# Moving the accumulation of two modulation vectors from the second attention to the expert query projection

## The reference, cut to what matters

```python
mod = cond @ ada_w[i] + ada_b[i]            # 1024 -> 6 * 1024
sh1, sc1, g1, sh2, sc2, g2 = jnp.split(mod, 6, axis=-1)
h = modulate_2(rms_norm_2(x, norm_g[i, 0]), sh1, sc1)      # h * (1 + scale) + shift
...
x = x + (1 + g1)[:, None, :] * rms_norm_2(y, norm_g[i, 1])
h = modulate_2(rms_norm_2(x, norm_g[i, 2]), sh2, sc2)
```

## Time and profile before

| | |
|---|---|
| median of 3 runs | 1780.07 us |
| the profiled execution | 1779.83 us |
| its span, first to last instruction | 1778.0 us |
| mean granted TensorE clock | 0.965 of full speed |
| PE busy | 1684.4 us, 95% of the span |
| DVE busy | 1225.7 us, 69% |
| ACT busy | 916.1 us, 52% |
| POOL busy | 567.1 us, 32% |
| read from device memory | 337.87 MB, 191 GB/s over the span |

### The profile page before, as it was taken

One profiled execution on the slowest core, in us unless ns is written; L12 is line 12 of the kernel. 1 busy time (PEld: TensorE's weight loads), 2 busy tenths in 40 slices (PEclk: granted clock), 3 DMA queues, 4 the chain that ended last, 5 costly groups with the idle time before them and its releaser, 6 DMA issues.

```text
span 1778.0 us, 32337 instructions
## 1 busy us (share of the span) xinstructions
PE 1684.4 (95%) x11292; PEld 1506.1 (85%) x11292; DVE 1225.7 (69%) x2236; ACT 916.1 (52%) x1747; POOL 567.1 (32%) x230
## 2 busy tenths in 40 slices
PE   2998899999999999999999999998899999789998
PEld 1985799999999998788888878966799999579997
DVE  5466508869808983877777767759578877646665
ACT  1445445455459994455455454257644445554443
POOL 0681278989985555000000005401310005130000
PEclk8899899999999999999999999888899998999999
DMA  8664455565553334988888664353477864035563
GB/s 326 220 208 166 143 185 171 179 182 181 181 177 116 118 108 159 325 288 286 288 293 291 209 194 125 106 209 124 154 240 278 279 219 142 25 119 179 188 189 107
DMA packets 98426, 341.14 MB, mean 192 GB/s; under 512 B 12147, under 2 KB 16003, under 8 KB 98340
## 3 DMA queue, kind: packets, MB, share of 16 engines
q1 hardware_dynamic: 93988, 336.01, 56.9%
q10 hardware_dynamic: 4352, 4.02, 0.7%
HBM read 337.87 MB, written 1.07 MB: 191 GB/s over the span
## 4 chain that ended last, share of the span: by engine, by line
PE 86%; DVE 6%; ACT 3%; DMA 3%; issue 2%; ACTq 0%; SPq 0%; DVEq 0%
PE banks L617 25%; PE banks L618 25%; PE banks L619 24%; PE banks L902 3%; DMA arena<-in_ada 1%; PE banks L784 1%; PE banks L758 1%; DMA ada_ring<-in_ada 1%; DVE arena L1577 1%; PE banks L797 1%; PE banks L681 1%; ACT arena L1233 1%; DVE arena L1684 1%; PE banks L741 1%; PE banks L688 1%
## 5 line engine op out<-in xcount | busy, mean ns | idle before, releaser
L570 POOL TENSOR_TENSOR weights_low<-ring,weights_high 128x1024 fp32r<-128x1024 f32 x226 | 566.9, 2519 | 1029.5 <-DVE ht_low L1652 625.8
L1194 ACT ACTIVATE weights_high<-ring 128x1024 fp32r<-128x1024 f32 x480 | 505.6, 1054 | 508.6 <-PE banks L619 479.5
L617 PE MATMUL banks<-ht_high,weights_high 128*128 128x256 f32 x2008 | 582.2, 290 | 8.2 <-DVE ht_low L1652 6.0
L618 PE MATMUL banks<-ht_low,weights_high 128*128 128x256 f32 x2008 | 571.9, 285 | 0.0
L619 PE MATMUL banks<-ht_high,weights_low 128*128 128x256 f32 x2008 | 571.7, 285 | 0.0
L617 PEld LDWEIGHTS banks<-ht_high,weights_high 128*128 128x128 f32 x2008 | 389.1, 194 | 14.0 <-issue 11.3
L618 PEld LDWEIGHTS banks<-ht_low,weights_high 128*128 128x128 f32 x2008 | 389.2, 194 | 2.7
L619 PEld LDWEIGHTS banks<-ht_high,weights_low 128*128 128x128 f32 x2008 | 388.6, 194 | 0.0
L1632 DVE TENSOR_TENSOR weights_low<-ring,weights_high 128x1024 fp32r<-128x1024 f32 x254 | 310.5, 1223 | 39.5 <-ACT weights_high L1194 34.4
L617 PE MATMUL banks<-weights_high,ga_parts 128*128 128x512 f32 x504 | 198.0, 393 | 6.5 <-DVE ga_parts L1935 6.5
L618 PE MATMUL banks<-weights_low,ga_parts 128*128 128x512 f32 x504 | 197.2, 391 | 0.0
(11 more groups left out here) (255 smaller groups left out, 2315.6 us busy)
## 6 DMA issues: line engine op xcount, KB each, us to landing
ring<-in_stream SPq DMA_DIRECT2D x490, 512.0 KB, 3.5
arena<-in_ada SPq DMA_DIRECT2D x88, 512.0 KB, 3.9
ada_ring<-in_ada SPq DMA_DIRECT2D x56, 512.0 KB, 4.4
arena<-bias_rows ACTq DMA_DIRECT2D x1, 2048.0 KB, 11.6
X<-in_x SPq DMA_DIRECT2D x1, 1024.0 KB, 6.1
out<-X SPq DMA_DIRECT2D x4, 256.0 KB, 2.0
arena<-arena ACTq DMA_DIRECT2D x8, 127.5 KB, 3.8
arena<-in_norm_final SPq DMA_DIRECT2D x1, 512.0 KB, 4.7
```

The costliest lines, as they stand in the source:

```text
L570: pool.tensor_tensor(WL[:, c % SLOTS, :], ring[:, c % SLOTS, :], WH[:, c % HIGHS, :], ALU.subtract)\
L617: pe.matmul(out, wh, xh, start=start, stop=False, **kw)
L618: pe.matmul(out, wh, xl, start=False, stop=False, **kw)
L1194: act.activation(WH[:, c % HIGHS, :], ring[:, c % SLOTS, :], ACT.Copy).then_inc(S["high_ready"], 1)
```

## The change

The 16 pieces of vectors 12 and 13 are loaded and added beside the projection `wq` instead of beside the second attention. SP issues one of them behind each chunk from the ninth on (`chunk["wq"] + SLOTS`), into the two slots `ADA_WQ`. DVE adds them in one run behind `shift_banks(1)` and in front of the first `top16`. PE sums both accumulators with `ada_columns` right behind the sub-key scores, with a wait on the last piece in front, and `mod_columns([12, 13], 3)` takes the sums behind DVE's last `top16` work. From `norm_transpose(3)` the call goes away. The accumulators and slots lie at other places of the arena, and the sums calls behind are renumbered, with their banks.

```diff
+ADA_WQ = [A_P, A_P + D]
+A_ACC_WQ = [A_XN, A_XN + D]
-ADA_BEFORE = dict(start=0, qk1=2 * DB, mixer1=3 * DB, out1=4 * DB, peer=5 * DB, layer2=6 * DB, mixer2=12 * DB, mlp2=14 * DB)
+ADA_BEFORE = dict(start=0, qk1=2 * DB, mixer1=3 * DB, out1=4 * DB, wq=5 * DB, peer=7 * DB, layer2=8 * DB, mlp2=14 * DB)
...
@@ SP @@
-            ahead = chunk["out1"] + SLOTS + 4
+            load_chunks(chunk["out1"] + SLOTS + 4, chunk["wq"] + SLOTS + 1)
+            for k in range(2 * DB):
+                load_ada(k, ADA_WQ, ADA_BEFORE["wq"] + k - 1 if k >= 2 else None, 12 * DB + k, "ada_wq")
+                load_chunk(chunk["wq"] + SLOTS + 1 + k)
+            ahead = chunk["wq"] + SLOTS + 1 + 2 * DB
...
-            for i in range(2 * DB):
-                load_ada(i, ADA_LAYER3, ADA_BEFORE["mixer2"] + i - 1 if i >= 2 else None, 12 * DB + i, "ada3_slot")
-                if 1 <= i <= SLOTS:
-                    load_chunk(chunk["out2"] + i - 1)
+            load_chunks(chunk["out2"], ahead)
...
@@ PE @@
+            pe.wait_ge(S["ada_used"], ADA_BEFORE["peer"])
+            ada_columns([A(first, D) for first in A_ACC_WQ], 3)
...
-            norm_transpose(3, lambda: summed_3(ADA_BEFORE["mlp2"], (12, 13), 6))
+            norm_transpose(3)
...
@@ DVE @@
+            for k in range(2 * DB):
+                ada_piece(k, ADA_BEFORE["wq"] + k, "ada_wq", ADA_WQ, A(A_ACC_WQ[k // DB], D), 1)
...
+            mod_columns([12, 13], 3)
...
-                if step % 3 != 2:
-                    i = step // 3 * 2 + step % 3
-                    ada_piece(i, ADA_BEFORE["mixer2"] + i, "ada3_slot", ADA_LAYER3, A(A_ACC3[12 + i // DB], D), 1)
...
-                mod_columns([[12, 13], [14, 17], [15, 16]][k], 6 + k)
+                if k:
+                    mod_columns([[14, 17], [15, 16]][k - 1], 6 + k)
```

More of the change, by code:

```diff
@@ L218 @@
 A_ACC2 = [(i + 1) * D for i in range(6)]
-A_ACC3 = {12: A_SPARE, 13: A_WIN + D, 15: A_WIN, 16: A_WIN + D, 14: A_WIN + 2 * D, 17: A_WIN + 3 * D}
+ADA_WQ = [A_P, A_P + D]
+A_ACC_WQ = [A_XN, A_XN + D]
+A_ACC3 = {15: A_WIN, 16: A_WIN + D, 14: A_WIN + 2 * D, 17: A_WIN + 3 * D}
 ADA_ORDER = [*range(14), 15, 16, 14, 17]
-ADA_ROWS = [A_Y, A_ACC + 5 * D, A_P, A_XN, A_P, A_P, A_P, A_P]
-ADA_BEFORE = dict(start=0, qk1=2 * DB, mixer1=3 * DB, out1=4 * DB, peer=5 * DB, layer2=6 * DB, mixer2=12 * DB, mlp2=14 * DB)
+ADA_ROWS = {0: A_Y, 1: A_ACC + 5 * D, 4: A_XN, 6: A_P}
+ADA_BEFORE = dict(start=0, qk1=2 * DB, mixer1=3 * DB, out1=4 * DB, wq=5 * DB, peer=7 * DB, layer2=8 * DB, mlp2=14 * DB)
 def two_blocks(nc, a):
@@ L349, in xt @@
             return banks[:, xt_bank(n, b), (b % 2) * T:(b % 2 + 1) * T]
-        SUM_BANK = {0: 5, 1: 5, 2: 7, 3: 5, 4: 7, 5: 3, 6: 7, 7: 7, 8: 6}
-        ROW_CALLS = [0, 1, 3, 5]
+        SUM_BANK = {0: 5, 1: 5, 2: 7, 3: 5, 4: 5, 5: 7, 6: 3, 7: 7, 8: 6}
+        ROW_CALLS = [0, 1, 4, 6]
         def gated(j):
@@ L867, in summed_1 @@
             def summed_1():
-                pe.wait_ge(S["ada_used"], ADA_BEFORE["peer"])
+                pe.wait_ge(S["ada_used"], ADA_BEFORE["wq"])
                 ada_columns([ACC1[:, v, :] for v in range(3, 5)], 2)
@@ L943, in _ @@
             pe.wait_ge(S["ada_used"], ADA_BEFORE["layer2"] + 6 * DB)
-            ada_rows([ada_acc[:]], 3)
+            ada_rows([ada_acc[:]], 4)
             for j in range(NKEYS - SLOTS, NKEYS - LEAD):
@@ L947, in _ @@
                 if j == NKEYS - 8:
-                    ada_turned(1, 3)
+                    ada_turned(1, 4)
                 if j == NKEYS - 5:
@@ L966, in rope @@
                     if u == 2:
-                        pe.wait_ge(S["mod_ready"], 6)
+                        pe.wait_ge(S["mod_ready"], 7)
                     x = RAW[:, raw % 3, :]
@@ L1035, in summed_2 @@
                 ada_row_half(layer2_rows, 2, 0)
-                ada_columns([A(first, D) for first in A_ACC2[:2]], 4)
+                ada_columns([A(first, D) for first in A_ACC2[:2]], 5)
             pe.wait_ge(S["gate_rows_taken"], 2)
@@ L1040, in _ @@
             pe.wait_ge(S["rope_loaded"], 16)
-            roped_product("nsa", 16, ROPES2, 0, 2, lambda: ada_turned(4, 5))
+            roped_product("nsa", 16, ROPES2, 0, 2, lambda: ada_turned(4, 6))
             for t in range(TT):
@@ L1435, in _ @@
                      NKEYS - 5: [NKEYS - 1]}
-            take_ada(1, 3)
+            take_ada(1, 4)
             for j in range(NKEYS - SLOTS, NKEYS - LEAD):
@@ L1455, in _ @@
             scaled(2)
-            take_ada(4, 5)
+            take_ada(4, 6)
             used(chunk["v"] + NKEYS - 1)
@@ L1994, in _ @@
                 if j == NKEYS - 7:
-                    mod_columns([5], 3)
+                    mod_columns([5], 4)
                     spread_gate(1)
@@ L2023, in rope @@
                     dve.tensor_tensor(dst(i), t1, t2, ALU.add).then_inc(S["rope_done"], 1)
-            mod_columns([6, 7], 4)
+            mod_columns([6, 7], 5)
             scale_column(2, branch_row(2))
@@ L2031, in _ @@
                 dve.tensor_scalar(X[:, t, :], ZN[:, t, :], small[:, 32 + t:33 + t], None, ALU.mult)
-            mod_columns([*range(8, 12)], 5)
+            mod_columns([*range(8, 12)], 6)
             scale_column(3, branch_row(3))
```

## The result

The changed kernel took 1787.5 us in the median of its first seven runs (1784.0 to 1792.9), the kernel before 1779.6 us (1774.4 to 1781.8) beside it. The ratio is 1.0048, with a 95% interval from 1.0029 to 1.0067: slower by 5 to 12 us, 8 us in the middle. Twelve more runs on another occasion gave 1787.2 us and 1.0046 (1.0026 to 1.0067), beside 1778.9 us. Single executions of one kernel spread by far more than the 1 or 2 us named ahead: the kernel before from 1772.4 to 1789.4 us in 35 runs of one occasion. The profiled execution took 1787.53 us, its span is 1785.7 us.

What follows compares the result with a forecast made beforehand. PE was taken to bound the kernel (86% of the span). Wait 7.3, sums 3.7 and clock 2.0, less 5.0 for the attention and 0 for normalisation 3, gave +8.0 us: 1788 us, range 1776 to 1797.

Steps and rivals of the forecast that it cites:

- the wait: Behind the sub-key scores, PE waits for the last piece's add, done at 280.3 us: 7.3 us, bounds 0 and 17.
- the clock: Behind the query projection, wait and sums with little matmul work lower PE's clock: 2.0 us lost, bounds 0 and 5.4.
- The attention: Second attention without the pieces: 3.4 us less waiting for DVE plus 1.6 us of clock, 5.0 us gained; bounds 1 and 12.4.
- Normalisation 3: The sums were hidden behind a wait for DVE's normalised rows, so removing them gives 0; range -0.5 to +1 us.
- the rival that they keep pace: Query projection: landing and adding stay under 5.76 us, so no wait and no clock fall; 1771 or 1776 us; chance 0.16.
- The formula for a transfer: Piece transfers: 2.0 us plus bytes at 436 GB/s, 3.2 us for 512 KB; the prediction let rows of 4.4 to 5.6 decide.
- an aside: Query projection: locking at every chunk makes POOL's 2.40 us plus 1.1 us slower than PE's 2.88, starving PE before the scores.
- both engines lock each other at every chunk: Query projection: DVE and POOL block each other, interval 4.1 us, wait 17.0 us; +18 to +21 us, 1799 us; chance 0.12.
- The sums: Between sub-key scores and experts, the moved sums stand unhidden on PE's path: +3.7 us in any case.
- The bound of 5.4 us: Upper limit for the loss by low clock behind the scores, with the sums themselves at half speed too.

Runs made afterwards that it cites:

- four slots: The changed kernel with four slots instead of two for the pieces beside the query projection; 1785.2 us, ratio 1.0024.
- the two with the sums in `u`: The changed kernel with the 32 sums 16 expert chunks later: PE's wait left behind the scores, 1787.4 us; wait moved with the sums, 1779.4 us.
- the early start: The changed kernel with four slots for the pieces and the first four loaded before the chunk loads that wait for the projection; 1780.8 us, ratio 1.0016.
- the low parts by DVE: The changed kernel with DVE making the low parts of all 16 query projection chunks, so POOL does nothing there; 1790.3 us, ratio 1.0057.

## Why the prediction was right, point by point

The forecast was +8.0 us and the result +8 us, but two of the terms were off in opposite directions: the wait by 3.2 us too much, the clock by 3.0 us too little. That they cancelled was luck; the path, a wait of PE for the last add, sums behind it and a fall of the clock, was foreseen.

**The attention, 5.0 forecast.** 5.0 us by the run with both vectors left out (1.4 to 8.5), 4.7 and 3.5 by the two profiles of the changed kernel. The mechanism held: the 3.4 us of the earlier trace rows became 0.9, and its long part went. The parts were sized a little otherwise: 2.5 us of wait and not 3.4, and the rest, 2.2 us of the 4.7, fits the clock, where I had guessed 1.6. Between the first scores' transposes and the last there were four low stretches before, 27.2 us, and three after, 20.4 us. Where they fall differs from one execution to the next: in the other profiles without a piece behind step 10 the way from the first transpose to normalisation 3 took from 99.0 to 104.2 us, against 106.3 in the one profile of the kernel before.

**Normalisation 3, 0 forecast.** PE idles 4.4 us there, and from its first transpose to the end it is 500.8 us in both.

**The wait, 7.3 forecast, 4.1 measured (4.3 in the second profile).** The mechanism was right, the size wrong, and this term was too large. The first add came at 229.9 instead of 225.8, but the scores came late by as much, which cancels. The interval was 3.35 us and not 3.5 (15 times 0.15 is 2.2 us), and the last add took 1.28 us and not 2.0, since POOL was idle by then. The 3.34 us of the earlier trace rows were the better row, though not for its reason: POOL did nothing there, and here it is DVE and POOL that set the interval. The transfers landed in 3.7 us in the median, less than the 4.4 us that I had taken as their shortest. By landing and adding alone, 3.7 and 1.28 us with two slots, the rival that they keep pace would have been right; four slots show that they did, and PE waited all the same. The formula for a transfer that the prediction quotes from the Trainium skill ("DMA: Bandwidth & Descriptors", section "Anatomy of one DMA") is fitted there to transfers issued by GpSimd, and these are issued by SP; they landed in 3.4 us at best, against the 3.2 us estimated from it.

**Who sets the pace.** The prediction worked out 2.40 us for POOL and 1.1 us of an add behind it, 3.5 us in all, but used it only for an aside. The 3.5 us of the sum came from two other rows, one without POOL and one with slots and landings, so that they met the pair's price was luck too. The pair was the whole matter: measured 3.35 us. The Trainium skill ("SBUF — State Buffer", section "SBUF: two separate sides") has the rule that a VectorE operation with two SBUF inputs and a GpSimd operation that reads SBUF lock each other out for a whole instruction. The trace agrees to within 0.3 us: 2.73 and 3.03 us each beside the other, 1.28 for an add with POOL idle, and 3.34 us a chunk when DVE always has one more, where 2.40 and 1.28 add up to 3.68. That rival, "both engines lock each other at every chunk", had the mechanism and missed the interval: it took 4.1 us, half of a landing of 5.5 us and a locked add of 2.73, and the landings were 3.7 us. And PE did not starve in the changed kernel, as the aside had it; it did when the adds began early.

**The sums, 3.7 forecast.** 3.5 to 3.6 us where the clock is full, and 2.3 to 3.4 us by the ratios of the runs that have them without a wait. In the changed kernel they took 6.25 us, of which 2.6 us belong to the next term.

**The clock, 2.0 forecast, 5 measured.** 2.6 us in the sums and 2.4 us in `u` (half of the 4.8 us from 287.73 to 292.50). This was the step that failed: I took the fall behind normalisation 1 for the size, 6.80 us with PE busy for 4.73, and the stretch was 10.2 us long and had matmul work on PE's path for all of its length. The bound of 5.4 us held it. I had the cause as "a wait and the sums" together; the runs show that the wait does it without the sums (8.4 us between the two versions that differ by it alone).

So 4.1 + 3.6 + 5.0 is 12.7 us, less 5.0 is 7.7 us, against 8.2 us by the ratio of the second comparison. The 13 us between leaving both vectors out and the changed kernel, which no profile enters, say the same.

**What stays open.** The scores began 4.1 and 4.3 us later in the two profiles of the changed kernel. All of it had come about by the first product of the projection (at 220.1 and 220.3 us instead of 216.1), in code that is the same, before the first of the moved transfers is issued at 225.5 us. In the first pair 2.5 us lie before normalisation 1, where the clock was low for 13.7 us instead of 10.2, and 1.5 us behind it, where it was low for 10.2 instead of 6.8 us. In the ten profiles of the experiments the first transposes of normalisation 1 came between 207.0 and 211.5 us, early with and without the pieces, late with and without them, though more often late with them. The second part is not so loose. From there to the first product of the projection it took 9.3 to 9.7 us in five profiles, both of the changed kernel, four slots, and the two with the sums in `u`, and 7.9 us in all seven others, the early start and the low parts by DVE among them. In the five the clock fell 2.0 to 2.5 us after the start of the sums of normalisation 1 and stayed low for 10.2 us, in the others 4.1 us or more after it and for 6.8 us. What decides that, and whether it is the edit, I do not know. The ratios leave 0.5 us for it (13.2 us between the changed kernel and both vectors left out, of which 12.7 lie between the first score and the gates), with intervals of several us. I tried nothing that would settle it.

## What to carry to other kernels

Work that moves to an idle engine is to be priced by what it shares with the engine beside it: here DVE was idle and the pair DVE and POOL was not. An add of 1.3 us and a low part of 2.4 us took the pair 3.35 us, where PE left it 2.88 for each chunk; with a piece at every second chunk, where it had 5.76, the add cost nothing. And a wait on the path of a busy PE can cost more than its length: here 4.1 us cost 9, since the clock fell and half speed held for 10 us of work behind it. Before a group of work is moved as a whole, look which of its members stand where the engine is late; here eight of sixteen did, and moving those eight was worth more than moving all.

## What the runs showed of the hardware that I had not expected

- The sums of both vectors, one-column matmuls (32 records), right behind the scores without a wait, ran at the full clock in all three profiles that have them so (3.5 to 3.6 us); behind them it stayed full in one and was low for 3.4 us in two. In the middle of `u` a low stretch of 3.4 us followed them in one profile, and one of 6.8 us began inside them in another. With a wait of 3.4 to 5.0 us in front, in four profiles, it was 6.8 to 10.2 us.
- With PE's wait of 5.0 us the clock fell before the wait was over (at 281.8 us, the wait ended at 284.5); with those of 4.1, 4.3 and 3.4 us it fell 0.8, 1.0 and 1.9 us after the sums had begun.
- With DVE never idle, a low part and an add together took 3.34 us, a little less than the sum of the two alone (2.40 and 1.28 us).
- The multiplication without a second input, 0.75 us alone (229.89 us), also took 2.65 us beside POOL (at 256.61 us in the changed kernel).
- A 512 KB transfer landed in 3.4 us at best with a chunk's transfer just ahead of it and another behind, in a stretch that moved 297 GB/s; beside `v` at 323 GB/s it was 4.9 us at best.
